# Last norm's second half transposed before it is normed, FFN seams re-ordered, first stage re-cut (one-core decoder trunk)

## The chip, the cores and the metric

One Trainium2 chip, one of its cores. The metric is the device time of one execution in microseconds (us). Engines: PE (TensorE, matrix products and transposes), ACT (ScalarE), DVE (VectorE), POOL (GpSimd) and SP (SyncE, which here only issues DMAs). PE runs at one of two clock levels, 2.4 GHz or 1.2 GHz; the profile gives the granted clock as a share, 1.00 or 0.50.

## The reference

A trunk of two layers over 512 tokens of width 1024, with a memory of 256 rows. Each layer is an FFN half-step, a mixer with cross-attention to the memory, and a second FFN half-step, each followed by a layer norm; so there are four FFNs.

```
def layer_norm(x, g, b):
    mu = jnp.mean(xf, -1, keepdims=True)
    var = jnp.mean(jnp.square(xf - mu), -1, keepdims=True)
    return ((xf - mu) * lax.rsqrt(var + LN_EPS) * g + b)
def swiglu(x, w_gu, w_down):
    a, b = jnp.split(x @ w_gu, 2, axis=-1)
    return (jax.nn.silu(a) * b) @ w_down
for i in range(DEPTH):
    x = layer_norm(ALPHA * x + 0.5 * swiglu(x, ffn1_w_gu[i], ffn1_w_down[i]), ln_g[i, 0], ln_b[i, 0])
    y, qm = gla_mix(...) if i == 0 else conv_mix(...)
    m = mem_attention(qm, mem, mem_w_kv[i])        # k, v = split(mem @ w_kv)
    x = layer_norm(ALPHA * x + jnp.concatenate([y, m], axis=-1) @ w_out, ln_g[i, 1], ln_b[i, 1])
    x = layer_norm(ALPHA * x + 0.5 * swiglu(x, ffn2_w_gu[i], ffn2_w_down[i]), ln_g[i, 2], ln_b[i, 2])
```

## The kernel before

**Layout and precision.** Activations lie with the channel on the partitions and the 512 tokens along the free axis (`u`, 8 blocks of 128 channels). Each f32 operand is split into a rounded high part (ACT casts it: `whi`, `xhi`, `h_hi`) and a low part, the difference (DVE or POOL: `wlo`, `xlo`, `h_lo`), and a product is three matmuls: high by high, low by high, high by low.

**Weights** come in numbered chunks through two slots of `raw`. For a chunk SP issues the load, ACT casts `whi` (`split_hi`, L547), DVE subtracts `wlo` (`split_lo`, L957), PE multiplies. The semaphores `hi_ready`, `lo_ready` and `w_used` count chunks. Every engine works its own instruction list in order.

**First stage.** SP loads `mem`, the first two chunks of `mem_w_kv`, `x`, some small parameter tables (`rows_in`, `dw_in`), and then the other six chunks of `mem_w_kv` as slots come free. PE transposes `mem` (16 transposes, L1716), ACT copies and casts it (L720, L722), POOL makes `mem_lo` (L476). Then PE works eight chunks of keys and values, 48 matmuls of 256 columns each; after chunk 0 and after chunk 1 it transposes four blocks of `x` each (`x_part`, L1727), which ACT copies out and casts (L714, L716). In ACT's list the cast of chunk 2's weights stands ahead of the copies of the first four blocks of `x`, and PE's second `x_part` waits for these copies (`tr_evac`), since they free its banks. The values come out with channels on partitions, so that after the FFN's first chunk PE transposes them back (`kv_values`, L1761) and ACT copies them (L743) before it issues the stores of keys and values to DRAM.

**FFN seam.** The down projection makes 1024 output channels in four pairs of blocks, p = 0 to 3, each from four weight chunks c = 0 to 3 (4, 4, 7 and 7 blocks of 128 deep). When a pair is done, DVE adds it to the scaled residual, block d = 2p and then d = 2p + 1 (`residual_pair`: L1012 scales, L1031 adds the product, L989 sums, L997 adds ACT's square), and only then makes `wlo` of the next pair's chunk c = 1. The last pair is worked in halves of 256 tokens, h = 0 in banks 0 and 1, h = 1 in banks 2 and 3 (`down_halves`). Before the second half's first chunk PE waits until DVE has read the pair p = 2 out of banks 2 and 3 (`y_evac` at 6).

**The end.** For each half of tokens: PE sums columns (L1478, L1487), DVE makes mean and variance (L1143 to L1152), POOL the reciprocal root, DVE centres eight blocks (L1155) and scales them (L1160) by a value spread over the partitions by PE (L1496), ACT applies gain and offset (L641), PE transposes to token rows (L2006), ACT or DVE copies to `out_tok` (L938, L1420), SP stores in 16 DMAs of 128 KB (L420, L426).

## Time and profile before

| | |
|---|---|
| median of 3 runs | 2138.03 us (2136.85 to 2140.4) |
| the profiled execution | 2137.1 us, span 2135.2 us |
| PE busy | 2092.3 us, 98% of the span |
| DVE, ACT, POOL busy | 972.6, 690.0, 238.0 us |
| chain that ended last | PE 88%, DVE 5%, ACT 3%, issue 2% |

How to read it: the chain follows the work back from the last instruction to what released it. A PE share of 88% says that most of the time a stretch is worth what PE does in it; the other parts of the chain are the places where PE waits or is done.

### The profile page before, as it was taken

The page shows a single profiled execution, that of the slowest core. Times are in us where ns is not written, and L with a number is a line of the kernel's source. Part 1 is how long each engine was busy: PE and PEld are TensorE (multiplying, and loading weights), DVE is VectorE, ACT ScalarE, POOL GpSimd, SP SyncE. Part 2 cuts the span into 40 slices and gives each one's busy share as a digit, 9 for nine tenths or more (in the row PEclk, how much of TensorE's full clock was granted, in tenths as well). Part 3 has the DMA queues.
Part 4 walks back from the last instruction along what each step waited for, and adds up shares of the span by engine and source line. Part 5 has one row for each costly group of instructions (what it writes and reads, how often), then busy time and mean ns, then how long its engine had stood idle before and what let it go on. Part 6 is the DMA issues. An engine that isn't in the chain of part 4 may idle for free.

```text
span 2135.2 us, 27022 instructions
## 1 busy us (share of the span) xinstructions
PE 2092.3 (98%) x10917; PEld 1784.6 (84%) x10917; DVE 972.6 (46%) x1299; ACT 690.0 (32%) x940; POOL 238.0 (11%) x170
## 2 busy tenths in 40 slices
PE   8999999999999999999999999999999899999998
PEld 7888888888987988888898888889887698888887
DVE  2333333443435833333363433336899773333235
ACT  5322222263433343322233333214342433222213
POOL 4121000043313210000011000002000321000000
PEclk9999999999999999999999999999999899999999
DMA  6644322332212234433233343332533222222231
GB/s 214 224 138 157 98 75 90 112 101 79 67 34 79 95 114 138 157 118 101 93 113 125 132 148 116 101 109 97 198 141 130 85 74 95 92 90 87 81 109 58
DMA packets 207167, 238.22 MB, mean 112 GB/s; under 512 B 5679, under 2 KB 199341, under 8 KB 205036
## 3 DMA queue, kind: packets, MB, share of 16 engines
q1 hardware_dynamic: 206444, 234.89, 32.9%
q10 hardware_dynamic: 640, 2.16, 0.2%
q8 instruction: 59, 0.97, 0.2%
q14 instruction: 24, 0.20, 0.0%
HBM read 215.02 MB, written 22.02 MB: 111 GB/s over the span
## 4 chain that ended last, share of the span: by engine, by line
PE 88%; DVE 5%; ACT 3%; issue 2%; DMA 1%; POOL 1%; ACTq 0%; POOLq 0%; SPq 0%; DVEq 0%
PE bank L1429 23%; PE bank L1430 23%; PE bank L1431 23%; PE bank L1436 3%; PE bank L1437 3%; PE bank L1438 3%; DVE u L1366 2%; PE bank L1507 1%; ACT u L641 1%; PE bank L1791 1%; PE bank L1790 1%; PE bank L1789 1%; DVE u L1155 1%; PE bank L1512 1%; POOL xlo L454 1%
## 5 line engine op out<-in xcount | busy, mean ns | idle before, releaser
L547 ACT CAST whi<-raw 128x2048 fp32r<-128x2048 f32 (+3 forms) x194 | 330.1, 1702 | 1082.5 <-PE bank L1431 975.5
L957 DVE TENSOR_TENSOR wlo<-raw,whi 128x2048 fp32r<-128x2048 f32 (+2 forms) x168 | 342.9, 2041 | 584.9 <-ACT whi L547 574.0
L1429 PE MATMUL bank<-xhi,whi 128*128 128x512 f32 x1552 | 607.7, 392 | 0.0
L1430 PE MATMUL bank<-xlo,whi 128*128 128x512 f32 x1552 | 604.6, 390 | 0.0
L1431 PE MATMUL bank<-xhi,wlo 128*128 128x512 f32 x1552 | 604.5, 389 | 0.0
L1429 PEld LDWEIGHTS bank<-xhi,whi 128*128 128x128 f32 x1552 | 291.6, 188 | 62.5 <-issue 2.1
L1431 PEld LDWEIGHTS bank<-xhi,wlo 128*128 128x128 f32 x1552 | 291.7, 188 | 61.0
L1430 PEld LDWEIGHTS bank<-xlo,whi 128*128 128x128 f32 x1552 | 291.8, 188 | 60.2 <-issue 0.5
L1429 PE MATMUL bank<-h_hi,whi 128*128 128x512 f32 x528 | 208.0, 394 | 3.3 <-DVE wlo L957 3.3
L1431 PE MATMUL bank<-h_hi,wlo 128*128 128x512 f32 x528 | 205.5, 389 | 0.0
L1430 PE MATMUL bank<-h_lo,whi 128*128 128x512 f32 x528 | 205.5, 389 | 0.0
L965 DVE TENSOR_TENSOR scratch<-scratch,bank 128x512 f32<-128x512 f32 x88 | 56.6, 685 | 273.5 <-PE bank L1431 269.0
L460 POOL TENSOR_TENSOR tiny<-tiny 128x2 f32<-128x2 f32 (+1 forms) x13 | 9.4, 722 | 1482.2 <-DVE tiny L1152 1482.2
L1429 PEld LDWEIGHTS bank<-h_hi,whi 128*128 128x128 f32 x528 | 99.1, 188 | 27.7 <-DVE wlo L957 6.5
L1366 DVE SCALAR_TENSOR_TENSOR u<-conv_in,w_dw,u 128x512 f32<-128x512 f32 x180 | 120.5, 746 | 0.0
L1430 PEld LDWEIGHTS bank<-h_lo,whi 128*128 128x128 f32 x528 | 99.1, 188 | 21.2 <-issue 1.0
L1431 PEld LDWEIGHTS bank<-h_hi,wlo 128*128 128x128 f32 x528 | 99.1, 188 | 20.7
L437 POOL TENSOR_TENSOR wlo<-raw,whi 128x2048 fp32r<-128x2048 f32 (+1 forms) x17 | 73.6, 4331 | 170.6 <-ACT whi L547 170.6
L454 POOL TENSOR_TENSOR xlo<-u,xhi 128x256 fp32r<-128x256 f32 (+1 forms) x88 | 80.0, 921 | 78.8 <-ACT xhi L637 62.0
L641 ACT ACTIVATE u<-u,prm 128x256 f32<-128x256 f32 (+1 forms) x104 | 60.7, 611 | 68.3 <-DVE u L1160 68.3
L1436 PE MATMUL bank<-h_hi,whi 128*128 128x256 f32 x240 | 68.9, 287 | 3.8 <-DVE u L1031 3.8
L1437 PE MATMUL bank<-h_lo,whi 128*128 128x256 f32 x240 | 67.9, 283 | 0.0
(296 smaller groups left out, 2910.9 us busy)
## 6 DMA issues: line engine op xcount, KB each, us to landing
raw<-in_ffn_w_gu_dram SPq DMA_DIRECT2D x88, 1024.0 KB, 4.9
raw<-in_ffn_w_down_dram SPq DMA_DIRECT2D x32, 896.0 KB, 4.4
raw<-in_ffn_w_down_dram SPq DMA_DIRECT2D x32, 512.0 KB, 3.4
raw<-in_gla_w_in_dram SPq DMA_DIRECT2D x14, 1024.0 KB, 5.1
raw<-in_conv_w_in_dram SPq DMA_DIRECT2D x10, 1024.0 KB, 5.3
early_raw<-in_conv_w_in_dram SPq DMA_DIRECT2D x18, 512.0 KB, 5.3
...
```

Of the source, the lines that this page charges most:

```text
L437: nc.gpsimd.tensor_tensor(wlo[:, s, 0:kc, 0:width], raw[:, s, 0:kc, 0:width], whi[:, s, 0:kc, 0:width].bitcast(F32), ALU.subtract).then_in ...
L454: nc.gpsimd.tensor_tensor(lo[:, k, tok], u[:, k, tok], hi[:, k, tok].bitcast(F32), ALU.subtract).then_inc(x_ready, 1)
L547: nc.scalar.copy(whi[:, s, 0:kc, 0:width], raw[:, s, 0:kc, 0:width]).then_inc(hi_ready, 1)
L641: nc.scalar.activation(u[:, k, tok], u[:, k, tok], func, scale=prm[:, g_row + k:g_row + k + 1], bias=prm[:, b_row + k:b_row + k + 1]).then ...
L957: nc.vector.tensor_tensor(wlo[:, s, 0:kc, 0:width], raw[:, s, 0:kc, 0:width], whi[:, s, 0:kc, 0:width].bitcast(F32), ALU.subtract).then_in ...
L1366: nc.vector.scalar_tensor_tensor(out=u[:, c, :], in0=src, scalar=w, in1=u[:, c, :], op0=ALU.mult, op1=ALU.add).then_inc(taps_done, 1)
L1429: nc.tensor.matmul(to, whi[:, s, k, w], hi, start=start, stop=False)
L1430: nc.tensor.matmul(to, whi[:, s, k, w], lo, start=False, stop=False)
L1431: return nc.tensor.matmul(to, wlo[:, s, k, w], hi, start=False, stop=stop)
L1436: nc.tensor.matmul(to[:, tok], w_hi[:, k, w], hi[:, k_in, tok], start=start, stop=False, skip_group_check=True)
L1437: nc.tensor.matmul(to[:, tok], w_hi[:, k, w], lo[:, k_in, tok], start=False, stop=False, skip_group_check=True)
L1438: return nc.tensor.matmul(to[:, tok], w_lo[:, k, w], hi[:, k_in, tok], start=False, stop=stop, skip_group_check=True)
```

## The change

1. **FFN seams.** In the pairs p = 0 to 2 DVE makes `wlo` of the next pair's chunk c = 1 between the two blocks of the residual (the argument `between`), instead of behind both. The last pair's second half of tokens goes to banks 6 and 4, and PE waits for `y_evac` at 2 there, instead of 6.
2. **First stage.** `mem` is loaded in two halves; PE does ten 128-column products of `ones` before it has data; ACT casts `mem_hi` straight from the bank; DVE, not POOL, makes `mem_lo`; chunk 0's weights are split in two halves; the value chunks are multiplied with memory rows as the stationary side, so they come out with rows on partitions, and the 16 transposes and 4 copies of `kv_values` go away.
3. **The end.** The second half of the tokens is transposed as it is (`rows`, 16 transposes), before its norm. DVE then subtracts the row's mean and multiplies by the gain (four instructions over 128x512 from the bank), and multiplies by the reciprocal root and adds the offset (four more). Gain and offset come over all partitions by four new DMAs. The first half's transposes stand behind these and are copied out four at a time by ACT; the second half is stored in 4 DMAs of 256 KB instead of 8 of 128 KB.

```
-DOWN_BANKS = [(6, 7), (0, 1), (2, 3), ((0, 1), (2, 3))]
+DOWN_BANKS = [(6, 7), (0, 1), (2, 3), ((0, 1), (6, 4))]
 OUT_BANKS = [(0, 1), (2, 3), ((0, 1, 2, 3), (0, 1, 2, 3))]
-FIN_BANK = [0, 1, 4, 6]
+FIN_BANK = [7, 6, 4, 7]
+ROW_BANK = [(2, 3), (0, 1)]
...
-            sp.dma_start(mem_in[:, :, :], a["mem"][0].rearrange("(b p) d -> p b d", p=P)).then_inc(mem_loaded, 16)
+            mem = a["mem"][0].rearrange("(b p) d -> p b d", p=P)
+            for i in range(2):
+                sp.dma_start(mem_in[:, :, i * 512:(i + 1) * 512], mem[:, :, i * 512:(i + 1) * 512]).then_inc(mem_loaded[i], 16)
...
+            sp.wait_ge(h_done, 4 * FK)
+            sp.wait_ge(res_done, RES_BASE[LN_FFN[3]] + DK)
+            for name, tiles in (("ln_g", gain), ("ln_b", offset)):
+                for j in range(2):
+                    row = a[name][DEPTH - 1, 2, 512 * j:512 * j + 512]
+                    sp.dma_start(tiles[j], row.partition_broadcast(P)).then_inc(gain_loaded, 16)
             to = out[0].rearrange("(b p) d -> p b d", p=P)
             for k in range(DK):
-                sp.wait_ge(fin_act, k + 1)
+                sp.wait_ge(fin_act, k // 2 + 1)
                 sp.dma_start(to[:, 0:2, k * P:(k + 1) * P], out_tok[:, k, 0:2, :]).then_inc(out_stored, 16)
-            for k in range(DK):
-                if k < 4:
-                    sp.wait_ge(fin_dve, k + 1)
-                else:
-                    sp.wait_ge(fin_act, DK + k - 3)
-                sp.dma_start(to[:, 2:4, k * P:(k + 1) * P], out_tok[:, k, 2:4, :]).then_inc(out_stored, 16)
-            sp.wait_ge(out_stored, 16 * 2 * DK)
+            for n in range(4):
+                j, b = divmod(n, 2)
+                sp.wait_ge(fin_dve, n + 1)
+                sp.dma_start(to[:, 2 + b, 512 * j:512 * j + 512], out_tok[:, 4 * j:4 * j + 4, 2 + b, :]).then_inc(out_stored, 16)
+            sp.wait_ge(out_stored, 16 * (DK + 4))
...
-                nc.scalar.copy(kv_t[:, 0, k, :], bank[4 + k % 4][:, 0:NMEM]).then_inc(mem_hi_ready, 1)
-                act.wait_ge(mem_hi_ready, 2 * k + 1)
-                nc.scalar.copy(mem_hi[:, k, :], kv_t[:, 0, k, :]).then_inc(mem_hi_ready, 1)
-                if k % 4 == 3:
-                    split_hi(0, k // 4)
+                nc.scalar.copy(mem_hi[:, k, :], bank[4 + k % 4][:, 0:NMEM]).then_inc(mem_hi_ready, 1)
+                if k in (3, 5):
+                    half = slice(0, 4) if k == 3 else slice(4, 8)
+                    act.wait_ge(raw_loaded[0], 16)
+                    nc.scalar.copy(whi[:, 0, half, :], raw[:, 0, half, :]).then_inc(first_hi if k == 3 else hi_ready, 1)
+            split_hi(0, 1)
             for n in range(8):
                 act.wait_ge(w_used, n + 1)
                 split_hi(n // 2 + 1, n % 2)
                 for t in range(2):
-                    if n == 0 and t == 0:
-                        act.wait_ge(mem_ready, DK)
-                    nc.scalar.copy(kv_t[:, n // 4, 2 * (n % 4) + t, :], bank[2 * (n % 2) + t][:, 0:NMEM]).then_inc(kv_evac, 1)
+                    c = n % 4
+                    to = kv_t[:, n // 4, 2 * c + t, :] if c < 2 else kv_v[:, n // 4, t, (c - 2) * 256:(c - 1) * 256]
+                    nc.scalar.copy(to, bank[2 * (n % 2) + t][:, 0:NMEM]).then_inc(kv_evac, 1)
...
-            for j in range(4):
-                act.wait_ge(kvv_done, j + 1)
-                nc.scalar.copy(kv_v[:, j // 2, j % 2, :], bank[4 + j][:, :]).then_inc(kvv_evac, 1)
-            act.wait_ge(kvv_evac, 4)
+            act.wait_ge(kv_evac, 16)
...
+            for i in range(4):
+                act.wait_ge(fin_mm, i + 1)
+                nc.scalar.copy(out_pairs[:, 2 * i:2 * i + 2, 0:2 * P],
+                               bank[FIN_BANK[i]][:, :].rearrange("p (k r) -> p k r", k=2)).then_inc(fin_act, 1)
...
-            def residual_pair(ln, p, n_used, coef, banks):
+            def residual_pair(ln, p, n_used, coef, banks, between=None):
 
                 for t in range(2):
                     d = 2 * p + t
+                    if t == 1 and between is not None:
+                        split_lo(*between)
                     if t == 1 and p:
                         add_square(ln, d - 1, 0)
...
                         split_lo(n0 + 4 * p + 4, 0, DOWN_K[0])
-                        residual_pair(ln, p, n0 + 4 * p + 4, 0.5, DOWN_BANKS[p])
-                        split_lo(n0 + 4 * p + 5, 1, DOWN_K[1])
+                        residual_pair(ln, p, n0 + 4 * p + 4, 0.5, DOWN_BANKS[p], (n0 + 4 * p + 5, 1, DOWN_K[1]))
...
+            def last_rows(ln):
+
+                unit = UNIT[ln] + 1
+                statistics(ln, 1)
+                dve.wait_ge(gain_loaded, 64)
+                for n in range(4):
+                    j, b = divmod(n, 2)
+                    dve.wait_ge(fin_rows, n + 1)
+                    nc.vector.scalar_tensor_tensor(out=out_tok[:, 4 * j:4 * j + 4, 2 + b, :],
+                                                   in0=bank[ROW_BANK[b][j]][:, :].rearrange("p (k e) -> p k e", k=4),
+                                                   scalar=mean_sq[:, 4 + b:5 + b], in1=gain[j].rearrange("p (k e) -> p k e", k=4),
+                                                   op0=ALU.subtract, op1=ALU.mult).then_inc(rows_centred, 1)
+                dve.wait_ge(rs_ready, unit + 1)
+                for n in range(4):
+                    j, b = divmod(n, 2)
+                    rows = out_tok[:, 4 * j:4 * j + 4, 2 + b, :]
+                    dve.wait_ge(rows_centred, n + 1)
+                    nc.vector.scalar_tensor_tensor(out=rows, in0=rows, scalar=rs[:, 2 + b:3 + b],
+                                                   in1=offset[j].rearrange("p (k e) -> p k e", k=4),
+                                                   op0=ALU.mult, op1=ALU.add).then_inc(fin_dve, 1)
...
+            def mem_low(ks):
+                for k in ks:
+                    dve.wait_ge(mem_hi_ready, k + 1)
+                    nc.vector.tensor_tensor(mem_lo[:, k, :], bank[4 + k % 4][:, 0:NMEM], mem_hi[:, k, :].bitcast(F32),
+                                            ALU.subtract).then_inc(mem_ready, 1)
+
+            mem_low(range(4))
+            dve.wait_ge(first_hi, 1)
+            nc.vector.tensor_tensor(wlo[:, 0, 0:4, :], raw[:, 0, 0:4, :], whi[:, 0, 0:4, :].bitcast(F32),
+                                    ALU.subtract).then_inc(first_lo, 1)
+            mem_low(range(4, 6))
+            dve.wait_ge(hi_ready, 1)
+            nc.vector.tensor_tensor(wlo[:, 0, 4:8, :], raw[:, 0, 4:8, :], whi[:, 0, 4:8, :].bitcast(F32),
+                                    ALU.subtract).then_inc(lo_ready, 1)
+            mem_low(range(6, 8))
+            for n in range(1, 10):
...
-                        pe.wait_ge(y_evac, Y_BASE[ln] + (6 if h else 4))
+                        pe.wait_ge(y_evac, Y_BASE[ln] + (2 if h else 4))
...
+            pe.wait_ge(consts, 1)
+            for _ in range(10):
+                nc.tensor.matmul(bank[0][:, 0:P], ones[:, :], ones[:, :], start=True, stop=True)
...
-            def to_tokens(h, ks):
+            def rows(ks):
+
                 for k in ks:
...

How the change moves instructions, at three places. First DVE in the first FFN, around the residual of pair p = 1: the first `wlo` is chunk c = 0 of pair 2, the last two are its chunks c = 2 and 3 (`scratch` holds the sums and squares). Before:

```order
L957 TENSOR_TENSOR wlo<-raw,whi 128x1024
L1012 SCALAR_TENSOR_TENSOR u<-u,scratch 128x512
L1031 SCALAR_TENSOR_TENSOR u<-bank,u 128x512
L989 TENSOR_TENSOR scratch<-scratch,u 128x512
L997 TENSOR_TENSOR scratch<-scratch 128x512
L1012 SCALAR_TENSOR_TENSOR u<-u,scratch 128x512
L1031 SCALAR_TENSOR_TENSOR u<-bank,u 128x512
L989 TENSOR_TENSOR scratch<-scratch,u 128x512
L997 TENSOR_TENSOR scratch<-scratch 128x512
L957 TENSOR_TENSOR wlo<-raw,whi 128x1024
L957 TENSOR_TENSOR wlo<-raw,whi 128x1792 x2
```

And the same place of the changed kernel:

```order
L957 TENSOR_TENSOR wlo<-raw,whi 128x1024
L1012 SCALAR_TENSOR_TENSOR u<-u,scratch 128x512
L1033 SCALAR_TENSOR_TENSOR u<-bank,u 128x512
L989 TENSOR_TENSOR scratch<-scratch,u 128x512
L957 TENSOR_TENSOR wlo<-raw,whi 128x1024
L997 TENSOR_TENSOR scratch<-scratch 128x512
L1012 SCALAR_TENSOR_TENSOR u<-u,scratch 128x512
L1033 SCALAR_TENSOR_TENSOR u<-bank,u 128x512
L989 TENSOR_TENSOR scratch<-scratch,u 128x512
L997 TENSOR_TENSOR scratch<-scratch 128x512
L957 TENSOR_TENSOR wlo<-raw,whi 128x1792 x2
```

The second 128x1024 `wlo`, chunk c = 1 of pair 2, moved up past five instructions of the residual.

Second, DVE at the very start, before the FFN's first products. Of the change:

```order
L1247 TENSOR_TENSOR mem_lo<-bank,mem_hi 128x256 x4
L1252 TENSOR_TENSOR wlo<-raw,whi 128x1024
L1247 TENSOR_TENSOR mem_lo<-bank,mem_hi 128x256 x2
L1256 TENSOR_TENSOR wlo<-raw,whi 128x1024
L1247 TENSOR_TENSOR mem_lo<-bank,mem_hi 128x256 x2
L957 TENSOR_TENSOR wlo<-raw,whi 128x2048 x10
```

Where the eleven 128x2048 `wlo` stood alone, the first is now two halves with the eight low parts of `mem` around them.

Third, PE behind the last product of the last down projection. Before:

```order
L2006 MATMUL bank<-ident,u 128x128 x4
L1478 MATMUL bank<-scratch,ones 128x256
L1487 MATMUL bank<-ones,scratch 128x1 x4
L2006 MATMUL bank<-ident,u 128x128 x12
L1496 MATMUL bank<-scratch,ones 128x256
L2006 MATMUL bank<-ident,u 128x128 x16
```

And the same place of the changed kernel (L2054 is in `rows`, L2071 in `to_tokens`):

```order
L2054 MATMUL bank<-ident,u 128x128 x8
L1528 MATMUL bank<-ones,scratch 128x1 x4
L2054 MATMUL bank<-ident,u 128x128 x8
L2071 MATMUL bank<-ident,u 128x128 x16
```

The two products that spread mean and reciprocal root over the partitions are gone, the second half's 16 transposes stand first, and the first half's 16 last.

## Rows read from the trace of the kernel before

**Rows 1.** The page: busy time, share of the span and instructions of each engine.
```profile
PE 2092.3 (98%) x10917; PEld 1784.6 (84%) x10917; DVE 972.6 (46%) x1299; ACT 690.0 (32%) x940; POOL 238.0 (11%) x170
```

**Rows 2.** Timeline of PE, then ACT, first stage: start, duration, engine, line, operation [idle before].
```profile
13.69 0.58 PE L1429 MATMUL bank<-mem_hi,whi 128*128 128x256 f32 x1 [3.92 <-DVE wlo L957]
...
31.95 0.66 PE L1727 MATMUL bank<-ident,xin 128*128 128x128 f32 x4 [0.48 <-ACT u L714]
32.36 0.36 PE L1429 MATMUL bank<-mem_hi,whi 128*128 128x256 f32 x1
...
25.55 1.91 ACT L547 CAST whi<-raw 128x2048 fp32r<-128x2048 f32 x1 [9.61 <-DMA raw<-in_mem_w_kv_dram]
```

**Rows 3.** Stretches: PE, PEld, DVE, ACT, POOL busy, clock, DMA share, GB/s; one DMA.
```profile
10.00:18.50 8.50, 4.81 (x22) 4.81 (x23) 4.76 (x2) 5.81 (x10) 4.51 (x5) 0.68 1.05 402
...
23.00:28.00 5.00, 5.00 (x45) 5.00 (x44) 0.51 (x1) 2.45 (x4) 0.00 (x0) 1.00 0.08 27
...
dw_in<-in_conv_w_dw_dram SPq DMA_DIRECT2D x1, 124.0 KB
```

**Rows 4.** Stretches, same columns: where the clock fell, and how long it stayed.
```profile
14.00:19.60 5.60, 5.60 (x27) 5.60 (x27) 2.47 (x1) 1.94 (x2) 2.29 (x4) 0.50 0.89 325
...
1651.20:1654.60 3.40, 0.99 (x4) 0.63 (x4) 3.40 (x6) 1.53 (x2) 0.00 (x0) 1.00 0.69 244
1654.60:1658.00 3.40, 3.40 (x11) 2.56 (x10) 3.33 (x6) 1.27 (x2) 0.00 (x0) 0.53 0.00 0
...
1695.60:1702.40 6.80, 5.89 (x12) 3.99 (x13) 3.80 (x7) 3.22 (x4) 0.00 (x0) 0.51 0.64 226
```

**Rows 5.** Timeline of PE: the transposes of the values.
```profile
78.81 1.91 PE L1761 MATMUL bank<-ident,kv_t 128*128 128x128 f32 x16
```

**Rows 6.** Timeline of PE at two seams of the first FFN.
```profile
375.03 0.39 PE L1430 MATMUL bank<-h_lo,whi 128*128 128x512 f32 x1
375.26 0.39 PE L1431 MATMUL bank<-h_hi,wlo 128*128 128x512 f32 x1
376.46 0.50 PE L1429 MATMUL bank<-h_hi,whi 128*128 128x512 f32 x1 [0.82 <-DVE wlo L957]
...
403.72 0.28 PE L1437 MATMUL bank<-h_lo,whi 128*128 128x256 f32 x1
403.84 0.28 PE L1438 MATMUL bank<-h_hi,wlo 128*128 128x256 f32 x1
405.07 0.36 PE L1436 MATMUL bank<-h_hi,whi 128*128 128x256 f32 x1 [0.95 <-DVE u L1031]
```

**Rows 7.** Timeline of ACT, then DVE, at the first of these seams.
```profile
370.24 1.05 ACT L547 CAST whi<-raw 128x1024 fp32r<-128x1024 f32 x1 [8.46 <-PE bank L1431]
...
373.19 0.69 DVE L1031 SCALAR_TENSOR_TENSOR u<-bank,u 128x512 f32<-128x512 f32 x1
...
375.19 1.22 DVE L957 TENSOR_TENSOR wlo<-raw,whi 128x1024 fp32r<-128x1024 f32 x1
```

**Rows 8.** Timeline of DVE, then ACT, at the end.
```profile
2118.20 0.42 DVE L1047 SCALAR_TENSOR_TENSOR u<-bank,u 128x256 f32<-128x256 f32 x1 [0.78 <-PE bank L1438]
...
2121.32 0.17 DVE L1152 TENSOR_SCALAR tiny<-tiny 128x2 f32<-128x2 f32 x1
...
2124.88 4.04 ACT L641 ACTIVATE u<-u,prm 128x256 f32<-128x256 f32 x8 [2.12 <-DVE u L1160]
```

**Rows 9.** SP's queue at the end: start and duration of an issue.
```profile
2120.82 0.39 SPq L420 DMA_DIRECT2D out_dram<-raw  x1
...
2128.46 2.31 SPq L426 DMA_DIRECT2D out_dram<-raw  x1
...
2132.93 0.50 SPq L426 DMA_DIRECT2D out_dram<-raw  x1
```

**Rows 10.** A stretch of the stores (columns as above); the stores and their time to landing.
```profile
2124.00:2124.50 0.50, 0.00 (x0) 0.00 (x0) 0.50 (x3) 0.00 (x0) 0.00 (x0) 1.00 0.81 241
...
out_dram<-raw SPq DMA_DIRECT2D x16, 128.0 KB, 1.9
```

134 lines of the change are left out of this document (73 added, 61 removed).

## The prediction

> **What bounds the kernel now.** I read the busy shares first: PE is busy in 98% of the span [rows 1], so only three things can give time: places where PE waits, work that PE need not do, and the ends where PE is not the last. Then I looked along PE's timeline for gaps near the changed code, and at each for what came last.
>
> At the start, PE waits 3.92 us for the first `wlo` and begins chunk 0 at 13.69. It begins chunk 2 at 32.36, right behind the last transposes of `x`, which had waited for ACT's copies [rows 2]. ACT could not copy earlier: its list has the cast of chunk 2's weights ahead of them, and that cast idled 9.61 us for a DMA, until 25.55 [rows 2]. From 10 to 18.5 the DMA engines are full, at 402 GB/s; from 23 to 28 they still work at a share of 0.08, about one engine of sixteen, at 27 GB/s, which in 5 us is 135 KB, close to the 124 KB of `dw_in` [rows 3]. So one engine is about 5 us behind the others, and what chunk 2 has on it lands last.
>
> At two seams of each FFN PE stops. At the first, matmuls start 0.23 us apart (375.03, 375.26), and the next starts at 376.46 instead of 375.49: 0.97 us lost to chunk c = 1's `wlo`. At the second they start 0.12 apart, and the next one starts at 405.07 instead of 403.96: 1.11 us lost to L1031 [rows 6]. The bracketed idle times, 0.82 and 0.95, are smaller, since they count from the modelled end of a matmul.
>
> At the end, DVE takes up the last product at 2118.20, the statistics are done at 2121.49, ACT begins the last affine at 2124.88 and needs 4.04 us for it [rows 8], and SP starts the last store at 2132.93 [rows 9]. That is 17.0 us from 2118.20 to the end of the span in which PE bounds nothing.
>
> **The change part by part.**
>
> *FFN seams.* The first seam: ACT has chunk c = 1 cast at 371.29, but DVE makes `wlo` only at 375.19, behind the second block of the residual [rows 7]. Moved up, it starts at about 371.35, takes 1.22 and is done at 372.6, 2.9 us before PE asks (375.49). DVE now waits in order for ACT's cast, and behind it stand the square's sum, the scaling and L1031 of the second block: they come about 0.7 us later (L1031 at 373.9 instead of 373.19). For the bank that L1031 reads, the next user is two pairs away; ACT's square of it stands before a cast that needs PE to finish a chunk at 375.5 anyway. If ACT's cast were 2.9 us later, this cover would be gone. The second seam: with banks 6 and 4 the second half waits for nothing late, and chunk c = 1's `wlo`, which it needs 2.9 us after that, has moved up as at the first. Next in line is the spare chunk c = 2, whose low part comes 0.5 to 1 us later than before, by about 410, while PE needs it at about 412.6 (four parts of 24 products at 0.12 from 401.1). Four FFNs have both seams: 4 x (0.97 + 1.11) = 8.3 us gain. The low bound goes by the idle times, 4 x (0.82 + 0.95) = 7.1. I take 8.3, as spacing is what PE loses.
>
> *Value transposes.* Sixteen transposes go, 1.91 us by the row, 1.8 us in starts (from 78.97, behind the last product, to the next chunk) [rows 5]. The value chunks keep their 48 matmuls of 256 columns. The four ACT copies had cover (PE's next chunk), and the key and value stores are issued some 10 us earlier, into a time with free DMA. Gain 1.8.
>
> *The rest of the first stage.* ACT loses eight copies before chunk 0, and chunk 0 can begin on half its weights: PE begins about 3 us earlier than 13.69. But chunk 2 comes when the late DMA engine has it, at 25.5, since the bytes ahead of it on that engine are the same. ACT is idle in between and then has the same list: chunk 2's cast, two evacuations, four blocks of `x`. So PE's last transposes of `x` again wait for ACT until about 32, and chunk 2 begins at 32.4 as before. The gain is nothing, and what is new is a hole: PE is done with chunk 1 near 26.5 and has only 16 transposes (1.8 us) until 32.4. A like hole, 0.99 us busy in 3.40, is followed by a stretch at a mean grant of 0.53, that is 1.2 GHz [rows 4]. Such stretches last 3.4 us (1654.6 to 1658.0), 5.6 (14.0 to 19.6) or 6.8 us (1695.6 to 1702.4) [rows 4]; half of it is lost. From chunk 2 on PE is the bound without a gap, so the loss stays. I take 4.6 us of low clock, a loss of 2.3; bounds 0 (no fall) and 3.4. The ten early products are before data arrives and cost nothing unless they run past the first half of `mem`; DVE's eight `mem_lo` stand where DVE was idle. Net of the first stage with the transposes: 0.5 us lost.
>
> The Trainium skill (DMA: Bandwidth & Descriptors, on why a semaphore goes up by 16) says that a DMA uses the largest number of engines up to 16 that divides its rows, so 31 rows go on one engine. The trace agrees (one engine of sixteen at work after 23, `dw_in` 124 KB), and by this rule the same engine is behind in the changed kernel; if chunk 2 came with the other engines, near 19, it could begin as soon as PE is free, and the first stage would gain some 4 us instead of losing 0.5.
>
> *The end.* Eight of the transposes stand ahead of the column sums now; PE idled there for DVE's sum of the last block, about one us behind 2118.20, so their 0.9 us (16 took 1.8) is hidden. Statistics are ready at 2121.49 or 0.3 earlier. Then DVE has eight instructions over 128x512, at 0.69 (L1031's, which also reads a bank) plus 0.03: 5.8 us, done at 2127.2, where before ACT's affine alone ended at 2128.92 [rows 7, 8]. The stores decide. The first half's first copy is 1.9 us later: eight row transposes behind the sums, to about 2121.6, four more (0.45), an ACT copy over 128x512 (0.6, estimated at half of what 128x1024 takes [rows 7], 1.05, and a start), so the first issue is at 2122.7 instead of 2120.82 [rows 9]. From there 2.1 MB go out at the 241 GB/s of these stores [rows 10], which all have pieces of 512 bytes: 8.7 us. With 0.8 from issue to first packet (1.9 to landing less 0.54 of transfer, and about 0.5 of completion) and 0.7 from the last packet to the end of the span: 2122.7 + 0.8 + 8.7 + 0.7 = 2132.9, 2.3 us before 2135.2. SP issues at 0.5 each, just as fast as they drain. The bounds: one issue took 2.31 us instead of 0.5 [rows 9], and one like it in the new row of stores takes the whole gain (0). If the stores with 2 KB on the DRAM side went at 402 GB/s, DVE would be the bound, and the end 2127.2 + 0.8 + 0.65 + 0.7 = 2129.4, a gain of 5.8. I take 2.3, since the pieces in SBUF stay at 512 bytes. The gain and offset loads have 15 us before they are read.
>
> **The sum.** 8.3 - 0.5 + 2.3 = 10.1 us. The profiled execution took 2137.1 us (span 2135.2), so it would be 2127.0; the median of the runs, 2138.0, lies 0.9 above it, which makes 2127.9.
>
> **The rivals.**
> - *The clock does not fall in the first stage, or chunk 2 comes earlier.* For it: 16 transposes are spread over the hole. Against it: 0.99 of 3.40 was too little. Time: 2127.9 - 2.3 = 2125.6. Chance 0.17.
> - *The stores run faster and DVE bounds the end.* For it: fewer and larger stores. Against it: 241 GB/s whenever the pieces are of 512 bytes. Time: 2127.9 - 3.5 = 2124.4. Chance 0.10. The Trainium skill (DMA: Bandwidth & Descriptors, Specifications) gives 512 bytes as enough for the line rate, which would bring this case; the trace's 241 against 402 GB/s contradicts it for stores.
> - *A slow issue in the last stores.* 2127.9 + 2.3 = 2130.2. Chance 0.08.
> - *A seam keeps its wait:* DVE, held in order by ACT, is late with something else, so that only one of the two is gained: 2127.9 + 4.4 = 2132.3. Against it are the 2.9 and 2.6 us of room. Chance 0.05.
> - *Slower than before.* The hole of the first stage leaves PE at 1.2 GHz, and it stays there through the six chunks to 68 and beyond. It decides from 14.4 us lost, that is 29 us at the low clock: 2142.4 and more. Against it: PE is full from 32.4 on, and the longest low stretch in the rows is 6.8 us. Chance 0.02.
>
> **How the numbers follow.** The forecast holds 0.58. All cases together reach from 2122.1 (8.3 + 1.8 + 5.8 gained) to 2132.5 (7.1 gained, 1.6 lost at the start); leaving a tenth on either side gives 2124.0 to 2131.5. This kernel's runs tell a change from none at about 0.2%, 4.3 us: faster is all below 2133.7, which is all but the last rival and a part of the one ahead of it for what else might meet it: 0.94, same 0.04, slower 0.02.
>
> **What would show it.** Right: no gap on PE at either seam; no L1761; chunk 2 begins near 32.4 with a clock of 0.50; the last DVE row instruction ends 9 us after the last product and the stores after it at 240 GB/s without a pause. Wrong: a new gap on PE behind the spare chunk; chunk 2 before 30; stores at 400 GB/s, or an issue of over 1 us; a low clock beyond 40 us.

## The result and the profile after

The changed kernel takes 2125.61 us (median, 2123.64 to 2126.47) against 2138.38 us (2136.85 to 2140.4) in the same series: a ratio of 0.9938, 95% interval 0.9921 to 0.9956. The forecast was 2127.9, its range 2124.0 to 2131.5. The profiled execution took 2125.7 us with a span of 2124.0, 11.2 less than before. One of the six executions of run 1 below took 2601.95 us and is left out of its numbers.

The page of the changed kernel, busy time, share and instructions, stands against [rows 1]:

```profile
PE 2091.7 (98%) x10917; PEld 1787.4 (84%) x10917; DVE 972.9 (46%) x1294; ACT 681.0 (32%) x913; POOL 230.6 (11%) x162
```

PE's busy time is as before. What went is idle time of PE, in the span's middle and at its end. To place it I use PE instructions that both kernels have as markers: each of the seven norms has one pair of products `bank<-u,ones`, which sums a block's shift. The starts of the seven pairs, and the last read of a half block by DVE (before: 2118.20 in [rows 8]):

```
                 FFN0    GLA out  FFN1     FFN2     conv     conv out FFN3     last read  span
before           338.98  689.13   1010.86  1380.55  1598.48  1696.51  2021.27  2118.20    2135.2
after            338.66  689.58   1011.33  1378.53  1593.98  1691.82  2015.99  2110.39    2124.0
after - before   -0.32   +0.45    +0.47    -2.02    -4.50    -4.69    -5.28    -7.81      -11.2
```

Each marker of an FFN lies ahead of the two seams, so an FFN's gain shows in the next column: 2.49, 2.48 and 2.53 us for FFN1, FFN2 and FFN3. FFN0's own gain, matmul by matmul from 338.07 to the seam at 405.07, is 2.48; the rest of the way to the next column then loses 3.25.

**Seams.** PE's timeline of the changed kernel where [rows 6] have the first gap, then DVE's and ACT's for [rows 7]:

```profile
374.46 0.39 PE L1470 MATMUL bank<-h_lo,whi 128*128 128x512 f32 x1
374.69 0.39 PE L1471 MATMUL bank<-h_hi,wlo 128*128 128x512 f32 x1
374.92 0.39 PE L1469 MATMUL bank<-h_hi,whi 128*128 128x512 f32 x1
...
370.76 1.22 DVE L957 TENSOR_TENSOR wlo<-raw,whi 128x1024 fp32r<-128x1024 f32 x1 [4.36 <-ACT whi L554]
...
373.23 0.69 DVE L1033 SCALAR_TENSOR_TENSOR u<-bank,u 128x512 f32<-128x512 f32 x1
...
369.68 1.06 ACT L554 CAST whi<-raw 128x1024 fp32r<-128x1024 f32 x1 [8.46 <-PE bank L1471]
```

Matmuls keep their 0.23 us through the seam (the chunk's first product is the one at 374.92), DVE's `wlo` starts with ACT's cast, and L1033 comes 0.04 later on the clock, some 0.6 relative to PE. The second seam reads the same, 0.12 us throughout.

**First stage.** Timeline of PE and ACT of the changed kernel, the place of [rows 2]:

```profile
11.81 0.55 PE L1469 MATMUL bank<-mem_hi,whi 128*128 128x256 f32 x1 [3.11 <-DVE wlo L1252]
...
29.25 0.63 PE L1772 MATMUL bank<-ident,xin 128*128 128x128 f32 x4 [1.52 <-ACT u L721]
...
31.43 2.25 PE L1772 MATMUL bank<-ident,xin 128*128 128x128 f32 x8 [0.48 <-ACT u L721]
33.34 0.56 PE L1803 MATMUL bank<-whi,mem_hi 128*128 128x256 f32 x1
...
26.18 1.91 ACT L554 CAST whi<-raw 128x2048 fp32r<-128x2048 f32 x1 [11.93 <-DMA raw<-in_mem_w_kv_dram]
```

A stretch of it (busy time of PE, PEld, DVE, ACT and POOL, then clock, DMA share, GB/s), for the first of [rows 3]:

```profile
10.00:18.00 8.00, 6.19 (x31) 6.22 (x32) 5.98 (x7) 4.24 (x7) 0.00 (x0) 0.57 1.05 402
```

PE starts chunk 0 at 11.81 instead of 13.69 and then comes to chunk 2 late all the same: ACT's idle time before the cast grew from 9.61 to 11.93, and the cast starts at 26.18.

**The end.** DVE, then ACT, then SP's queue, of the changed kernel, for [rows 8] and [rows 9]:

```profile
2110.39 0.42 DVE L1049 SCALAR_TENSOR_TENSOR u<-bank,u 128x256 f32<-128x256 f32 x1 [0.77 <-PE bank L1478]
...
2113.52 2.73 DVE L1165 SCALAR_TENSOR_TENSOR raw<-bank,tiny,scratch 128x512 f32<-128x512 f32 x4
2116.16 2.73 DVE L1174 SCALAR_TENSOR_TENSOR raw<-raw,tiny,scratch 128x512 f32<-128x512 f32 x4
...
2114.21 2.05 ACT L946 COPY raw<-bank 128x512 f32<-128x512 f32 x4 [1.47 <-PE bank L2071]
...
2114.82 4.12 SPq L433 DMA_DIRECT2D out_dram<-raw  x8
2118.99 2.31 SPq L437 DMA_DIRECT2D out_dram<-raw  x4
```

Two stretches of its stores, for [rows 10]:

```profile
2118.00:2120.00 2.00, 0.00 (x0) 0.00 (x0) 0.89 (x2) 0.00 (x0) 0.00 (x0) 0.99 0.84 249
2120.00:2122.00 2.00, 0.00 (x0) 0.00 (x0) 0.00 (x0) 0.00 (x0) 0.00 (x0) 0.50 1.10 331
```

From the last read to the end of the span it is 13.6 us (2124.0 - 2110.39) instead of 17.0. The first half's stores drain at 249 GB/s with the DMA engines at a share of 0.84; the second half's, four of 256 KB, at 331 with a share of 1.10.

**The loss in the mixer's stage.** Three stretches behind FFN0, of the kernel before:

```profile
464.00:468.00 4.00, 2.87 (x10) 1.11 (x9) 0.70 (x1) 2.69 (x3) 2.31 (x1) 1.00 0.68 235
468.00:472.00 4.00, 3.15 (x8) 1.66 (x7) 2.31 (x4) 3.98 (x6) 4.00 (x2) 0.80 0.12 16
472.00:476.00 4.00, 4.00 (x15) 3.19 (x15) 0.00 (x0) 3.97 (x6) 2.69 (x1) 0.77 0.75 249
```

And of the changed kernel:

```profile
464.00:468.00 4.00, 4.00 (x7) 1.61 (x6) 1.50 (x2) 3.06 (x3) 4.00 (x2) 0.56 0.00 1
468.00:472.00 4.00, 3.16 (x6) 1.34 (x5) 1.50 (x2) 2.05 (x3) 4.00 (x1) 0.50 0.79 245
472.00:476.00 4.00, 4.00 (x13) 3.21 (x12) 0.00 (x0) 3.97 (x6) 0.04 (x1) 0.66 0.72 215
```

The clock (third number from the right) stands at 1.2 GHz for 10.2 us after the change (464.5 to 474.7), for 3.4 us before. The change has no edit there; the two kernels only reach the place 2.8 us apart.

### The profile page after: what moved, and what is told of

Its sections match the earlier page's. It is cut to its first block, busy times and chain, and to the rows that moved or that the text cites. A ratio compares the mean times of both kernels' runs of the same rounds, so it can differ in the third digit from the quotient of the medians.

```text
span 2124.0 us, 26980 instructions
## 1 busy us (share of the span) xinstructions
PE 2091.7 (98%) x10917; PEld 1787.4 (84%) x10917; DVE 972.9 (46%) x1294; ACT 681.0 (32%) x913; POOL 230.6 (11%) x162
## 3 DMA queue, kind: packets, MB, share of 16 engines
q1 hardware_dynamic: 207228, 235.94, 33.3%
## 4 chain that ended last, share of the span: by engine, by line
PE 89%; DVE 5%; ACT 2%; DMA 1%; issue 1%; POOL 1%; SPq 0%; DVEq 0%; POOLq 0%; ACTq 0%
PE bank L1469 23%; PE bank L1470 23%; PE bank L1471 23%; PE bank L1476 3%; PE bank L1477 3%; PE bank L1478 3%; DVE u L1410 2%; PE bank L1548 1%; DMA raw<-in_mem_w_kv_dram 1%; PE bank L1841 1%; PE bank L1840 1%; PE bank L1839 1%; PE bank L1553 1%; POOL xlo L465 1%; PE bank L1722 1%
## 5 line engine op out<-in xcount | busy, mean ns | idle before, releaser
L554 ACT CAST whi<-raw 128x2048 fp32r<-128x2048 f32 (+2 forms) x193 | 328.6, 1703 | 1074.9 <-PE bank L1471 956.8
L957 DVE TENSOR_TENSOR wlo<-raw,whi 128x2048 fp32r<-128x2048 f32 (+2 forms) x167 | 339.8, 2035 | 596.3 <-ACT whi L554 585.4
L1469 PE MATMUL bank<-xhi,whi 128*128 128x512 f32 x1552 | 608.0, 392 | 0.0
L1471 PE MATMUL bank<-xhi,wlo 128*128 128x512 f32 x1552 | 604.7, 390 | 0.0
L1470 PE MATMUL bank<-xlo,whi 128*128 128x512 f32 x1552 | 604.5, 389 | 0.0
L1469 PEld LDWEIGHTS bank<-xhi,whi 128*128 128x128 f32 x1552 | 292.0, 188 | 62.3 <-issue 2.1
L1471 PEld LDWEIGHTS bank<-xhi,wlo 128*128 128x128 f32 x1552 | 291.7, 188 | 61.2
L1470 PEld LDWEIGHTS bank<-xlo,whi 128*128 128x128 f32 x1552 | 292.0, 188 | 60.1 <-issue 0.5
L1469 PE MATMUL bank<-h_hi,whi 128*128 128x512 f32 x528 | 207.0, 392 | 0.0
L1471 PE MATMUL bank<-h_hi,wlo 128*128 128x512 f32 x528 | 205.5, 389 | 0.0
L1470 PE MATMUL bank<-h_lo,whi 128*128 128x512 f32 x528 | 205.4, 389 | 0.0
L1470 PEld LDWEIGHTS bank<-h_lo,whi 128*128 128x128 f32 x528 | 99.1, 188 | 21.5 <-issue 1.0
L1469 PEld LDWEIGHTS bank<-h_hi,whi 128*128 128x128 f32 x528 | 99.1, 188 | 21.3 <-issue 1.0
L1471 PEld LDWEIGHTS bank<-h_hi,wlo 128*128 128x128 f32 x528 | 99.1, 188 | 20.7
L1478 PE MATMUL bank<-h_hi,wlo 128*128 128x256 f32 x240 | 67.9, 283 | 0.0
```

What stands on the lines that cost most here:

```text
L554: nc.scalar.copy(whi[:, s, 0:kc, 0:width], raw[:, s, 0:kc, 0:width]).then_inc(hi_ready, 1)
L957: nc.vector.tensor_tensor(wlo[:, s, 0:kc, 0:width], raw[:, s, 0:kc, 0:width], whi[:, s, 0:kc, 0:width].bitcast(F32), ALU.subtract).then_in ...
L1469: nc.tensor.matmul(to, whi[:, s, k, w], hi, start=start, stop=False)
L1470: nc.tensor.matmul(to, whi[:, s, k, w], lo, start=False, stop=False)
L1471: return nc.tensor.matmul(to, wlo[:, s, k, w], hi, start=False, stop=stop)
L1478: return nc.tensor.matmul(to[:, tok], w_lo[:, k, w], hi[:, k_in, tok], start=False, stop=stop, skip_group_check=True)
```

## The experiments

The theory: at the seams the two edits together take away PE's wait; the first stage is bounded by when chunk 2 lands; the end by the stores. Each run is named by what it changes. "After" is the changed kernel. Ratios are to the kernel before, which had medians of 2137.38 (runs 1 to 4), 2136.72 (5 to 8) and 2136.49 us (9 to 12).

**1. Seams alone** (before, with both edits of the seams, whose diffs stand at runs 4 and 12).

> The kernel before with only the seam edits: chunk c = 1's low part between the two residual blocks, the last pair's second half in banks 6 and 4, its wait at y_evac 2. Theory A (the seams carry most of the gain; three seams of each FFN, since the changed kernel also lost a restart of 0.23 us at the seam behind pair 0): 4 x (0.23 + 1.11 + 1.2), about 10 us faster, 2128 us. Rival B (the seams give what the idle times in brackets said, 4 x 1.77 = 7.1, and the rest of the 12.8 us comes from the first stage and the end): 2131 us.

2128.09 us, ratio 0.9959 (0.9946 to 0.9972), span 2126.2: theory A's number. From FFN1's marker to FFN2's it takes 367.17 us against 369.69 before, as the changed kernel (367.20). The seams are most of the change.

**2. The old end** (after, with part 3 of the change undone).

```
-            for n in range(4):
-                j, b = divmod(n, 2)
-                sp.wait_ge(fin_dve, n + 1)
-                sp.dma_start(to[:, 2 + b, 512 * j:512 * j + 512], out_tok[:, 4 * j:4 * j + 4, 2 + b, :]).then_inc(out_stored, 16)
+            for k in range(DK):
...
+                sp.dma_start(to[:, 2:4, k * P:(k + 1) * P], out_tok[:, k, 2:4, :]).then_inc(out_stored, 16)
...
-            rows(range(4))
-            sums(ln, 1, False)
-            rows(range(4, DK))
-            to_tokens()
+            to_tokens(0, range(2))
+            sums(ln, 1)
+            to_tokens(0, range(2, DK))
+            spread_rstd(ln, 1)
+            to_tokens(1, range(DK))
```

> The changed kernel with the end of before (norm of the second half on channels, affine on ACT, 16 stores of 128 KB); seams and first stage changed. Theory A (the end is worth the 3.4 us by which the stretch from the last product to the end of the span became shorter, 17.0 to 13.6): 3.4 us slower than the changed kernel, about 2129.0. Rival B (the end is worth the 2.3 us of the forecast): 2127.9. Rival C (the end gave more than the span shows, since it also moved the clock): over 2130.

2125.55 us, ratio 0.9948 (0.9935 to 0.9961), span 2125.8: by the median nothing is lost against the changed kernel (2125.61 in its own series), by the span 1.8 us, less than either theory said. SP's queue shows why:

```profile
2113.22 4.91 SPq L424 DMA_DIRECT2D out_dram<-raw  x8
2119.92 4.11 SPq L430 DMA_DIRECT2D out_dram<-raw  x8
```

Here the last eight issues take 4.11 us in all. The kernel before had 5.90, with the slow one of [rows 9]. In five traces with the old end, its length from the last read and this sum go together: 17.05 and 5.90, 16.59 and 5.45 (run 1), 16.34 and 5.19 (run 4), 15.75 and 4.60 (run 12), 15.26 and 4.11 here; the difference is 11.14 or 11.15 each time. So a slow issue in this row adds its own length, and against an old end without one the new end gains 15.26 - 13.58 = 1.7 us.

The traces also show what goes with a slow issue. DMA queues of the kernel before, 2128 to 2131 us, in which the issue of 2.31 us lies:

```profile
q1 hardware_dynamic: 523, 0.25, 29.2%
q8 instruction: 1, 0.02, 3.9%
```

The second line is the queue of instructions, one packet of 16 KB that takes 1.9 us from 2128.46, where the slow issue begins. All five traces with the old end have one slow issue (in run 2 it is in the first row, 4.91 us, where it costs nothing), and each overlaps such a packet. None of the nine with the new end has a slow issue, and in none does such a packet fall among the stores. Where it falls moves with the code, so a further edit could bring it back.

**3. The old first stage** (after, with part 2 of the change undone, the old value transposes included).

```
-            mem_low(range(4))
...
-            for n in range(1, 10):
+            for n in range(10):
...
-            ffn(0, values_read)
+            ffn(0, kv_values)
```

> The changed kernel with the first stage of before (memory loaded whole, low parts on POOL, values transposed back); seams and end changed. Theory A (the first stage gains 1.8 us by the transposes and loses 1.5 us up to chunk 2, net 0.3): within 1 us of the changed kernel, 2125 to 2127. Rival B (the first stage carries the 1.4 us by which the medians differ more than the two profiled runs): 2127.5 or more. Rival C (it costs time, through the hole and the clock): 2124 or less.

2123.59 us, ratio 0.9942 (0.9929 to 0.9955). FFN0's marker stands at 338.46 against 338.66: the new first stage is worth nothing. Over all traces the marker stands between 338.46 and 339.03 with the old first stage (five) and between 338.66 and 339.60 with the new one (changed kernel, runs 2 and 6). By the median this is rival C's case, but not by its cause. The span is 2.3 us shorter, and 2.7 of that is the mixer's stage, which has no edit between the two.

**4. Only `wlo` moved up** (before, with `between`, without the banks).

```
-                        residual_pair(ln, p, n0 + 4 * p + 4, 0.5, DOWN_BANKS[p])
-                        split_lo(n0 + 4 * p + 5, 1, DOWN_K[1])
+                        residual_pair(ln, p, n0 + 4 * p + 4, 0.5, DOWN_BANKS[p], (n0 + 4 * p + 5, 1, DOWN_K[1]))
```

> The kernel before with only the low part of chunk c = 1 moved between the residual blocks; banks and waits of before. Theory A (each seam's loss has its own cause): the seams behind pairs 0 and 1 go, 4 x (0.23 + 1.1) = 5.3 us; the one behind pair 2 stays, and grows by about 0.7 us each, since L1031 of the second block now comes 0.7 us later: 2.5 us net, about 2135.9. Rival B (the second seam does not grow): 5.3 us, 2133.1.

2134.54 us, ratio 0.9985 (0.9976 to 0.9994), near theory A. The first seam's wait is gone, and the second's has grown from 0.95 [rows 6] to 1.55, since DVE's L1033 now stands behind `wlo`. PE's, then DVE's timeline:

```profile
403.98 0.35 PE L1437 MATMUL bank<-h_hi,whi 128*128 128x256 f32 x1 [1.55 <-DVE u L1033]
...
403.14 0.69 DVE L1033 SCALAR_TENSOR_TENSOR u<-bank,u 128x512 f32<-128x512 f32 x1
```

Per FFN, matmul by matmul: -0.22 us behind pair 0, -1.15 behind pair 1, +0.60 behind pair 2, together -0.77.

**5. Small tables later** (after, with `load_parameters()` issued behind chunk 2's load).

```
                     if n == 1:
                         sp.dma_start(xin[:, :, :], a["x"][0].rearrange("(b p) d -> p b d", p=P)).then_inc(x_loaded, 16)
+                    if n == 2:
                         load_parameters()
```

> The changed kernel, with the loads of the small tables (dw_in, 124 KB on one DMA engine, and the parameter rows) issued behind the load of chunk 2 instead of ahead of it. Theory A (chunk 2's load is held only by the one DMA engine that works off the tables): chunk 2 is cast near 20 us instead of 26.2, the wait of PE for ACT's copies of x goes, chunk 2's products start near 29.5 instead of 33.3, and the kernel is about 4 us faster than the changed one (about 2121.5). Rival B (the load is late by the total of bytes, or by its issue): cast still near 26, time unchanged.

2118.37 us, ratio 0.9913 (0.9898 to 0.9928): 7 us less than after by the medians, which are of two series, 5.6 by the span (2118.4), 5.65 at FFN0's marker (333.01). ACT, then PE, for the rows shown above:

```profile
19.79 1.90 ACT L555 CAST whi<-raw 128x2048 fp32r<-128x2048 f32 x1 [5.68 <-DMA raw<-in_mem_w_kv_dram]
...
26.50 1.91 PE L1773 MATMUL bank<-ident,xin 128*128 128x128 f32 x16
```

Chunk 2 is cast 6.4 us earlier, and the 16 transposes of `x` run without a gap. SP issues its load at nearly the same time as in the changed kernel (13.35, 13.49), so what held it up is the work ahead of it on its engines. That is above all `dw_in`, 124 KB on one engine [rows 3]: 31 packets of 4 KB, which take 159 ns each, 4.9 us in all. The seven small loads of `rows_in`, 63 KB together, moved with it; the run doesn't tell them apart.

**6. First half stored wide** (after, with the first half of tokens in four stores of 256 KB).

```
-            for k in range(DK):
-                sp.wait_ge(fin_act, k // 2 + 1)
-                sp.dma_start(to[:, 0:2, k * P:(k + 1) * P], out_tok[:, k, 0:2, :]).then_inc(out_stored, 16)
+            for n in range(4):
+                j, b = divmod(n, 2)
+                sp.wait_ge(fin_act, 2 * j + 2)
+                sp.dma_start(to[:, b, 512 * j:512 * j + 512], out_tok[:, 4 * j:4 * j + 4, b, :]).then_inc(out_stored, 16)
...
-            sp.wait_ge(out_stored, 16 * (DK + 4))
+            sp.wait_ge(out_stored, 16 * 8)
```

> The changed kernel, with the first half of the tokens also stored in 4 DMAs of 256 KB with 2 KB runs in DRAM, instead of 8 of 128 KB with runs of 512 bytes. Theory A (the runs in DRAM set the rate of a store, 331 against 240 GB/s): the stretch from the last product to the end of the span, 13.6 us, falls by 0.5 to 1.1. Rival B (the rate of the last stores rose because they are larger or for lack of an issue bound): 0 to 0.5. Rival C (the first store must now wait for a second ACT copy, which costs more than the rate gives): longer by up to 0.6.

2123.72 us, ratio 0.994 (0.9927 to 0.9954), span 2121.9. The end is 12.8 us instead of 13.6, and the stores drain at 346 GB/s. SP's queue of this run:

```profile
2114.04 2.19 SPq L434 DMA_DIRECT2D out_dram<-raw  x4
2116.28 2.44 SPq L438 DMA_DIRECT2D out_dram<-raw  x4
```

A stretch of them:

```profile
2116.00:2118.00 2.00, 0.00 (x0) 0.00 (x0) 1.63 (x3) 0.00 (x0) 0.00 (x0) 1.00 1.15 346
```

The 0.8 us are theory A's number, but two things changed at once, the run in DRAM (512 bytes or 2 KB) and the bytes of an issue, and the rows speak for the second, the issue bound of rival B. In the changed kernel SP's eight issues of 128 KB take from 2114.82 to 2118.99, 1.05 MB in 4.17 us: 251 GB/s, the rate at which they drain. The stores and their time to landing there:

```profile
out_dram<-raw SPq DMA_DIRECT2D x8, 128.0 KB, 1.9
out_dram<-raw SPq DMA_DIRECT2D x4, 256.0 KB, 2.7
```

The 128 KB stores land 1.9 us behind their issue from the third to the last, so nothing queues up, and the DMA engines are at a share of 0.84. In this run four issues of 256 KB take 2.24 us, 468 GB/s, more than the engines move: the share is 1.15, and the time to landing grows from 2.2 to 3.4 us. Divided by the share, the rate is the same everywhere: 249/0.84 = 296, 331/1.10 = 301, 346/1.15 = 301. And in the packet records all stores are packets of 512 bytes with a median of 27 ns, whatever their run in DRAM. So with 128 KB stores the issues set the rate, and with 256 KB the engines. No run changes the DRAM run alone.

**7. Both** (runs 5 and 6 together).

> The changed kernel with the tables later and the wide stores. If both theories A hold: about 5 us faster than the changed kernel, 2120.5. If only the first: 2121.5.

2117.98 us (2115.47 to 2118.2), ratio 0.9908 (0.9893 to 0.9923), span 2116.5, not to be told from run 5. By the medians of two series it is 7.6 us below the changed kernel, by the span 7.5. The end is 12.8 us, as in run 6.

**8. No early products** (after, less three lines).

```
-            pe.wait_ge(consts, 1)
-            for _ in range(10):
-                nc.tensor.matmul(bank[0][:, 0:P], ones[:, :], ones[:, :], start=True, stop=True)
```

> The changed kernel without the ten products of ones at its start. Theory A (chunk 2 waits for its load, so nothing before it counts): no difference at chunk 2, and none in the time. Rival B (the early products bring the clock up for the first chunks, and that is worth something): 1 to 3 us slower than the changed kernel.

2125.21 us, ratio 0.9945 (0.9932 to 0.9959), theory A. Chunk 2's cast does not move (26.06), so the whole doesn't either. The stretch of the first chunks, and two products in it:

```profile
10.00:18.00 8.00, 6.34 (x35) 6.37 (x36) 5.98 (x7) 4.10 (x7) 0.00 (x0) 1.00 1.05 402
...
16.28 0.39 PE L1469 MATMUL bank<-mem_hi,whi 128*128 128x256 f32 x1
16.50 0.29 PE L1470 MATMUL bank<-mem_lo,whi 128*128 128x256 f32 x1
```

The clock in the first line, 1.00, is not what PE ran at: this trace has no record of the clock before 16.50, and up to there these products start 0.21 us apart, behind it 0.12. The changed kernel has 0.21 until 17.3. So the early products don't keep the first chunks from 1.2 GHz, and chunk 0 starts no earlier with them (11.81) than without (11.66).

**9. The hole before the second mixer's output norm filled** (both, and one line).

```
                 if p == 0:
+                    keep_busy(16, xhi[:, 0, 0:P], xhi[:, 0, :])
                     shift_sum(LN_CONV_OUT)
```

> The version with late small tables and wide stores, and in it sixteen further 128x512 products into a bank of which nothing is read, before the second layer's output norm is spread over the partitions, where PE idles 4.2 us (1680.90 to 1685.09) and a low-clock stretch of 6.8 us follows. Theory A: the clock falls because PE stands still there; with the hole filled it does not fall, and half of 6.8 us comes back: about 2114.6 against that version's 2118.0. Theory B: the low clock behind the hole comes from something else, or the products (16 x 0.22 = 3.5 us at 2.4 GHz, up to 7 at 1.2) run past the end of the hole: within 1 us of 2118, or later by up to 3.

`keep_busy(16, ...)` issues sixteen 128x512 products that nobody reads. 2117.47 us (2113.48 to 2119.26), ratio 0.9907 (0.9894 to 0.9921): the whole is not to be told from run 7, as theory B said. Theory A's mechanism holds in the section, its size does not. PE's timeline of run 7 at the hole:

```profile
1685.09 2.07 PE L1649 MATMUL bank<-u,ones 128*128 128x512 f32 x2 [4.19 <-DVE u L1035]
1686.17 1.41 PE L1471 MATMUL bank<-c_hi,whi 128*128 128x512 f32 x1
```

And of this run:

```profile
1682.20 3.79 PE L1654 MATMUL bank<-xhi 128*128 128x512 f32 x16
1686.61 1.12 PE L1649 MATMUL bank<-u,ones 128*128 128x512 f32 x2 [0.62 <-DVE u L1035]
1687.17 0.79 PE L1471 MATMUL bank<-c_hi,whi 128*128 128x512 f32 x1
```

No low clock follows, and from this marker to FFN3's it takes 321.89 us instead of 324.16: 2.3 gained, not 3.4, since part of the low stretch had lain in the hole, where nothing ran. The whole gained less, as the first mixer's stage, without an edit, took 2.8 us more (351.23 against 348.44).

**10. All holes of the convolution's stage filled** (run 9, and these).

```
+            keep_busy(9, xhi[:, 0, 0:P], xhi[:, 0, :])
             out_a(LN_CONV_OUT, CONV_OUT_N, 0, 1, mo_hi_c, mo_lo_c)
...
-            keep_busy(4, xhi[:, 0, 0:P], xhi[:, 0, :])
+            keep_busy(13, xhi[:, 0, 0:P], xhi[:, 0, :])
             spread_rstd(LN_CONV, 0)
-            keep_busy(4, xhi[:, 0, 0:P], xhi[:, 0, :])
+            keep_busy(11, xhi[:, 0, 0:P], xhi[:, 0, :])
```

> The same as the run before it, and further such products in the convolution stage's other holes (2.4, 2.4 and 2.0 us at 1640.2, 1658.8 and 1665.0): 13 and 11 in place of 4 and 4 around the norm of the convolution, and 9 more ahead of its output product. Theory A: all of that stage then stays at 2.4 GHz and gives back up to 5 us more, about 2110 to 2112. Theory B: a product issued in a stretch at 1.2 GHz takes 0.43 us instead of 0.22, so that the row runs past the hole and delays PE by what it gains: the same as the run before it, or 1 to 3 us slower.

2115.36 us (2115.35 to 2118.24), ratio 0.9901 (0.9886 to 0.9917), not to be told from run 9. The stage now runs at full clock throughout, and takes 97.92 us between its markers, as with 1.2 GHz in it (97.88 in run 7, 97.99 in run 9). The number is theory B's, but its reason falls with theory A: the clock stays up and nothing is gained. The stretch of the convolution's output in run 7:

```profile
1660.00:1676.00 16.00, 12.86 (x34) 9.09 (x35) 11.54 (x19) 11.24 (x18) 9.14 (x6) 0.59 0.14 49
```

And in this run:

```profile
1660.00:1676.00 16.00, 12.41 (x49) 8.71 (x48) 13.71 (x26) 9.91 (x16) 7.91 (x5) 1.00 0.16 48
```

PE does not set the end of this stage. The timeline of DVE, then POOL, of run 7 shows what does, and the last section reads it:

```profile
1678.97 2.59 DVE L1012 TENSOR_SCALAR u<-xlo 128x512 f32<-128x512 f32 x1 [7.43 <-POOL c_lo L467]
1681.59 2.71 DVE L1018 SCALAR_TENSOR_TENSOR u<-xhi,u 128x512 f32<-128x512 f32 x1
1684.34 0.69 DVE L1035 SCALAR_TENSOR_TENSOR u<-bank,u 128x512 f32<-128x512 f32 x1
...
1689.22 0.69 DVE L1018 SCALAR_TENSOR_TENSOR u<-xhi,u 128x512 f32<-128x512 f32 x1
...
1666.86 12.07 POOL L467 TENSOR_TENSOR c_lo<-u,c_hi 128x512 fp32r<-128x512 f32 x8 [7.21 <-ACT c_hi L646]
1678.89 4.86 POOL L459 TENSOR_TENSOR a_spare_c<-raw,a_spare_c 128x1024 fp32r<-128x1024 f32 x2
```

**11. The gates' entry filled** (both, and two lines).

```
             low_rank()
+            for _ in range(4):
+                nc.tensor.matmul(bank[7][:, :], xhi[:, 0, 0:P], xhi[:, 0, :], start=True, stop=True)
```

> The version with late small tables and wide stores, and in it four further 128x512 products into a bank that is free, ahead of the gates of the first layer's mixer, where a low-clock stretch of 6.8 to 10.2 us lies. Theory A: the clock falls there for what PE does just before, and 0.9 us of full products hold it up: 2 to 4 us less than 2118.0. Theory B: the low stretch belongs to the gate products themselves (short, with 32 rows or columns), which stay as they are: the four products only add their 0.9 us, 2118.9.

2115.28 us (2114.29 to 2115.69), ratio 0.9901 (0.9885 to 0.9916), span 2113.2. In the profiled execution there is no low clock at the gates, where each of the other 13 traces has 3.4 to 10.2 us:

```profile
459.00:466.00 7.00, 6.16 (x22) 3.74 (x21) 3.00 (x4) 6.29 (x8) 7.00 (x2) 1.00 0.38 115
```

From FFN0's marker to the next it takes 346.51 us, the least of all traces, against 348.44 in run 7. That speaks for theory A; the intervals of the two ratios overlap, so the gain (1.5 us by the ratios, 1.9 by the section, 2.7 by the medians) is likely and not settled.

**12. Banks alone** (before, with the banks and the wait, without `between`).

```
-DOWN_BANKS = [(6, 7), (0, 1), (2, 3), ((0, 1), (2, 3))]
+DOWN_BANKS = [(6, 7), (0, 1), (2, 3), ((0, 1), (6, 4))]
...
-                        pe.wait_ge(y_evac, Y_BASE[ln] + (6 if h else 4))
+                        pe.wait_ge(y_evac, Y_BASE[ln] + (2 if h else 4))
```

> The kernel before with nothing of the change but the banks of the second half of the last down pair (6 and 4, and the wait for two blocks of the residual in place of six). Theory A: the wait of 1.2 us (1.11 by the spacing of starts) at the second seam goes at each of the four FFNs, and chunk c = 1's low part, which PE asks for 2.9 us later, is made in time even in its old place: 4.4 to 4.8 us less, 2132.5 to 2133 against some 2137.3. Theory B: with the low part still in its old place the wait comes back 2.9 us later at that chunk, in part or whole: 2135 to 2137, and the timeline shows it as a new gap behind DVE's wlo.

2133.96 us, ratio 0.9991 (0.9982 to 1.0). PE passes the second seam and stops behind chunk c = 0, for the `wlo` that is still behind the residual (PE's timeline):

```profile
403.73 0.28 PE L1436 MATMUL bank<-h_hi,whi 128*128 128x256 f32 x1
...
407.27 0.39 PE L1436 MATMUL bank<-h_hi,whi 128*128 128x256 f32 x1 [0.50 <-DVE wlo L957]
```

The product behind a wait starts late, and so does the one after it. With both counted 1.18 us are gained and 0.78 come back, so an FFN keeps 0.40: theory B, in part. The runs 4 and 12 together save 0.77 + 0.40 = 1.2 us per FFN, and the two edits at once 2.5. Half of what the seams bring exists only with both.

## Why the prediction was right, and where it was off

- **Seams, 8.3 us forecast, 10.0 measured** (2.48 + 2.49 + 2.48 + 2.53 in the trace; run 1 has 9.3 by the medians). The mechanism held: no gap, `wlo` at 370.76 (forecast 371.35), the spare chunk in time. The term was mis-sized by 0.4 per FFN. Over half of that is a third seam that no bracket marks: behind pair 0, three products of the kernel before start at 345.09, 345.43 and 345.77, the same of the changed one at 344.77, 345.00 and 345.22, so 0.23 us are regained. The rest is the restart behind a wait, whose second product also comes late (0.34 and 0.19 instead of 0.23 and 0.12).
- **First stage, 0.5 us lost forecast, 0.3 gained measured.** What was forecast is there: chunk 2 still waits for its late part, the last transposes wait for ACT (chunk 2 at 33.3, forecast 32.4), and the clock behind is low. But that stretch was short, to 34.4, of which 1.1 us lie behind chunk 2's start: about half a microsecond lost instead of 2.3. Chunk 2 itself comes 1.0 us later instead: its cast came 0.6 later and the last eight transposes ran at 1.2 GHz (2.25 us). Chunk 0 began 1.9 us earlier, not 3, which by itself cost nothing. The 0.3 gained are no more than the scatter of the marker from trace to trace (run 3). The case in which chunk 2 comes with the other engines was rightly excluded, and run 5 shows what it would have been worth: 5.6 us, against the "some 4". The prediction's sizes of low stretches came from few rows: the one from 14.0 ran from 13.0 to 19.8, 6.8 us, and the kernel before has one of 10.2 us (1671.9 to 1682.1) that its rows don't show.
- **The end, 2.3 us forecast, 3.5 measured** (17.05 less 13.58). The first issue came 4.4 us behind the last read, as worked out (4.5). The term that was mis-sized is the drain of the stores: the second half's 1.05 MB go at 331 GB/s, not 241, which is 1.2 us less. The step that failed is "I take 2.3, since the pieces in SBUF stay at 512 bytes": 241 GB/s was not the rate of 512-byte pieces but of 128 KB per issue, and the prediction had both halves of it in hand ("SP issues at 0.5 each, just as fast as they drain"). With 256 KB per issue the same pieces drain at 331 to 346 (run 6). How much of the 3.5 belongs to the change is a second question: the kernel before had a slow issue of 2.31 us in this execution, so 1.8 are its absence and 1.7 remain. Against the five traces with the old end, 15.26 to 17.05 us, on average 16.2, the new end gains 2.6.
- **Not foreseen: 3.25 us lost in the first mixer's stage**, by a longer stretch at 1.2 GHz. No edit of the change lies there, and among kernels that all have both seam edits and the same code from FFN0's marker to the next, that section took 348.25 us with 6.8 us of low clock in it (run 3), 348.94 with 10.2 (run 6), 350.92 with 13.7 (the changed kernel), 350.97 with 13.7 (run 8) and 352.08 with 17.1 (run 10). The kernel before had 6.8 and, without the loss at its seams, 347.67. So the time goes with how long the clock stands at 1.2 GHz in it; why an execution gets more or less of that stays open, and with one trace of each kernel it isn't shown that the change has no part in it.
- **The sum.** -0.3 at the start, -10.0 at the seams, +3.25, -0.8 around the convolution and -3.5 at the end are -11.3, the 11.2 of the span. The forecast of 10.1 was close partly by luck: seams, end, first stage and convolution gave 4.5 us more than forecast, and the low clock took 3.25 back. By the median the gain is 12.8. The measured 2125.61 lies within the range given.
